# Two layers of 32 experts on one core: experts with one block mixed evenly among those with more, and the overflow loop in two passes behind another expert

## The chip, the core and the metric

The kernel runs on one NeuronCore of a Trainium2 chip. The metric is the device time of one execution in microseconds (us). The core has five engines that are named here by the profile's names: PE (TensorE, with PEld for its weight loads), DVE (VectorE), ACT (ScalarE), POOL (GpSimd) and SP (SyncE, which here issues the large DMA transfers). Each has its own instruction stream; they wait for each other on semaphores.

## The reference

The program is a trunk of two layers on 512 tokens of width 1024, all in float32. Each layer has a mixer (attention in layer 0, a gated linear recurrence in layer 1) and then a mixture of 32 experts of which every token takes two. This change touches only the expert part, which is this:

```python
def moe(xt, idx, wts, w_gu, w_dn):          # xt 512 x 1024, w_gu 32 x 1024 x 1024, w_dn 32 x 512 x 1024
    ...
    def expert_block(args):                 # a block: rows of tokens that chose expert e
        xb, e = args
        g, u = jnp.split(xb @ w_gu[e], 2, axis=-1)
        return (jax.nn.silu(g) * u) @ w_dn[e]
    ...
    return jnp.einsum('tk,tkd->td', wts.astype(y.dtype), y)
```

## The kernel before

**Blocks.** The kernel works in blocks of 32 rows. A fixed plan of 60 blocks per layer gives each expert a number of blocks before the tokens are known: `CAP` gives it by rank. Ranks 0 to 3 are experts 0 to 3 with two blocks each; the other experts are ranked by their number of tokens, and rank 4 has five blocks, rank 5 four, ranks 6 to 8 three, ranks 9 to 19 two, and ranks 20 to 31 one. `RUN` is the order in which the ranks are worked on; a rank's position in it is called its place (0 to 31) here. The blocks are numbered 0 to 59 in that order.

**Work of a block on PE.** Gate and up projections (L1155, 64 matmuls in the trace), the addition to the tokens for a block four earlier (L1182, 32 matmuls), and the down projection of the block before (L1162, 32 matmuls). With each third block of four come 8 transposes of the next four blocks' rows (L1146). Each matmul has a weight load beside it on PEld. The function that does this is the loop over `n` behind `more_blocks()` in the tensor block; ACT, DVE and POOL have loops of the same shape. POOL gathers the rows of four blocks at a time (L714).

**Weights.** An expert's weights are 4 MB (gate and up, "GU") and 2 MB (down, "DN"). There are three sets of buffers, and place n uses set n % 3: set 0 is `ring_gu1`/`ring_dn0`, set 1 `ring_gu0`/`ring_dn1`, set 2 lies in `arena`. `load_expert(n)` on SP (L597 for GU, L599 for DN) waits until the last block of place n - 3 is done with the buffer, and then issues the load. SP issues in the order of the places, all on one DMA queue, GU and DN by turns. A block whose expert has not landed is waited for by PE.

**The overflow loop.** An expert with more tokens than its blocks hold is finished in extra blocks, at most 28, in a loop that all five engines run at one point of the plan: behind block `MORE_BLOCK`, where the buffers of place `MORE_PLACE` = 12 are free (set 0). The count `n_more` is read from memory; an outer loop steps over groups of four extra blocks, and an `If` skips a group that isn't needed. After it, PE counts `more_pe` up, and only then does SP issue the load of place 15. In the profiled execution no extra block ran: the page lists 44 GU loads into `ring_gu` and 18 into `arena`, which are those of 31 places of each layer; place 2 is loaded in parts, and nothing comes on top.

Of the kernel before, what the change touches and what calls it, by code (L numbers as in the profile page):

```python
# [44 lines left out]
MAX_EXTRA = 28  # L45
GROUP = 4
# [6 lines left out]
HEAVY = 20  # L53
# [8 lines left out]
def column(o, j):  # L62
# [3 lines left out]

RUN = ([0, 1, 2, 3, 20, 9, 21, 8, 22, 10, 23, 7, 24, 11, 25, 5, 26, 12, 27, 4, 6]
       + list(range(13, HEAVY)) + [28, 29, 30, 31])
BLOCKS = [(o, j) for o in RUN for j in range(CAP[o])]
NB = len(BLOCKS)  # L70
NU = NB // TILES
assert sorted(RUN) == list(range(NE)) and NB == NU * TILES == sum(CAP)
assert max(column(o, j) for o, j in BLOCKS) < OVCOL
# [15 lines left out]
MORE_PLACE = 12  # L89
MORE_UNIT = 5  # L90
MORE_SET = MORE_UNIT % 2
MORE_BLOCK = TILES * MORE_UNIT + TILES - 1
# [93 lines left out]
def trunk(nc, x, c, positions, norm_mix, norm_ffn, w_ada, b_ada, mla_w_in, mla_q_a_norm, mla_kv_a_norm,  # L186
# [4 lines left out]
    with ctx:  # L191
# [308 lines left out]
        def _(sp):  # L500
# [39 lines left out]
            for l in range(2):  # L540
# [69 lines left out]
                sp.wait_ge(S["dn_done"], gone(MORE_PLACE, l))  # L610
                with sp.Fori(0, MAX_EXTRA // GROUP) as group:
                    with sp.If(n_more > group * GROUP):
                        with sp.Fori(group * GROUP, group * GROUP + GROUP) as u:
                            e = sp.value_load(more_i[0:1, bass.ds(u, 1)], min_val=0, max_val=NE - 1)
                            sp.wait_ge(o["dn_done"], u + 1)
                            sp.dma_start(GU[0].rearrange("p k n -> p (k n)"), gu_rows(l, e)).then_inc(o["w_in"], 16)
                            sp.dma_start(DN[0].rearrange("p k n -> p (k n)"), dn_rows(l, e)).then_inc(o["w_in"], 16)
# [16 lines left out]
        def _(pool):  # L634
# [58 lines left out]
            for l in range(2):  # L693
# [29 lines left out]
                n_more = pool.value_load(more_i[0:1, 31:32], min_val=0, max_val=MAX_EXTRA)  # L723
                with pool.Fori(0, MAX_EXTRA // GROUP) as group:
                    with pool.If(n_more > group * GROUP):
                        with pool.Fori(group * GROUP, group * GROUP + GROUP) as u:
                            g.tensor_copy(idx_in[0:ROWS, :], tok_idx[0:ROWS, bass.ds(u + OVCOL, 1)]).then_inc(o["idx"], 1)
# [13 lines left out]
        def _(pe):  # L741
# [283 lines left out]
            for l in range(2):  # L1025
# [177 lines left out]
                def more_blocks():  # L1203
                    o = OV[l]
                    pe.wait_ge(S["more_ready"], l + 1)
                    n_more = pe.value_load(more_i[0:1, 31:32], min_val=0, max_val=MAX_EXTRA)
                    with pe.Fori(0, MAX_EXTRA // GROUP) as group:
                        with pe.If(n_more > group * GROUP):
                            with pe.Fori(group * GROUP, group * GROUP + GROUP) as u:
                                pe.wait_ge(o["gathered"], u * 16 + 16)  # L1210
# [70 lines left out]
        def _(act):  # L1281
# [181 lines left out]
            for l in range(2):  # L1463
# [93 lines left out]
                u = 2 * l + 1  # L1557
# [34 lines left out]
                def more_blocks():  # L1592
# [3 lines left out]
                    n_more = act.value_load(more_i[0:1, 31:32], min_val=0, max_val=MAX_EXTRA)  # L1596
                    with act.Fori(0, MAX_EXTRA // GROUP) as group:
                        with act.If(n_more > group * GROUP):
                            with act.Fori(group * GROUP, group * GROUP + GROUP) as ub:
                                act.wait_ge(o["xT_made"], ub + 1)  # L1600
# [26 lines left out]
        def _(dve):  # L1627
# [364 lines left out]
            for l in range(2):  # L1992
# [81 lines left out]
                u = 2 * l + 1  # L2074
# [201 lines left out]
                def more_blocks():  # L2276
                    o = OV[l]
                    dve.wait_ge(S["more_ready"], l + 1)
                    n_more = dve.value_load(more_i[0:1, 31:32], min_val=0, max_val=MAX_EXTRA)
                    with dve.Fori(0, MAX_EXTRA // GROUP) as group:  # L2280
                        with dve.If(n_more > group * GROUP):
                            with dve.Fori(group * GROUP, group * GROUP + GROUP) as ub:
                                dve.wait_ge(o["sil"], ub + 1)
# [100 lines left out]
```

## Time and profile before

| | us |
|---|---|
| median of 3 runs | 1695.38 |
| the three runs | 1690.26, 1695.38, 1696.04 |
| profiled execution, own time | 1690.38 |
| its span | 1688.6 |
| expert part of layer 0, about | 400 to 914 of the span |
| expert part of layer 1, about | 1183 to 1688 of the span |

The profile is of one execution; all times of rows are from the start of its span. The profiled execution's time is 1.8 us more than its span, and 5.0 us less than the median.

### The profile page before, as it was taken

To read this page: it belongs to the slowest core of one execution; us is meant where nothing else is said; L and a number is where in the kernel's file an instruction comes from. 1 tells how busy PE (TensorE), PEld (TensorE's weight loads), DVE (VectorE), ACT (ScalarE), POOL (GpSimd) and SP (SyncE) were. 2 spreads that over 40 slices of the span, in tenths; PEclk is the share of its full clock that TensorE was granted. 3 is DMA by queue.
4 is the path that set the end of the run, shared out by engine and by line. 5 is a ranking of instruction groups with operands and counts; after the bars stand their busy time and mean duration, and the time that the engine had idled before them with its cause. 6 is when DMAs were issued, how large, how long until landed. Compare 5 with 4: busy or idle time off the path is not lost.

```text
span 1688.6 us, 40579 instructions
## 1 busy us (share of the span) xinstructions
PE 1545.8 (92%) x17779; PEld 894.6 (53%) x17779; DVE 974.5 (58%) x1632; ACT 349.0 (21%) x708; POOL 175.9 (10%) x212
## 2 busy tenths in 40 slices
PE   3999999989998869899998999897999889899997
PEld 2654555445565536566655444343566446566664
DVE  4677777666555325455555378756565435455555
ACT  2346555131100001001002144613100000000100
POOL 1002211000101001001000122200010000100100
PEclk9999999989999989999999999998999989999999
DMA  9553332499999989979996122047799999998995
GB/s 363 232 231 141 109 98 89 158 345 389 386 401 404 407 319 395 402 309 394 413 429 240 50 75 75 25 187 311 308 404 387 403 399 408 397 353 356 407 424 240
DMA packets 59959, 500.96 MB, mean 297 GB/s; under 512 B 9557, under 2 KB 22290, under 8 KB 43146
## 3 DMA queue, kind: packets, MB, share of 16 engines
q1 hardware_dynamic: 50544, 485.38, 72.4%
q0 software_dynamic: 5088, 7.81, 1.5%
q10 hardware_dynamic: 4154, 5.18, 0.9%
q8 instruction: 143, 2.34, 0.6%
q14 instruction: 30, 0.25, 0.0%
HBM read 497.89 MB, written 6.32 MB: 299 GB/s over the span
## 4 chain that ended last, share of the span: by engine, by line
PE 77%; DMA 11%; DVE 7%; issue 2%; ACT 2%; SPq 1%; DVEq 0%; ACTq 0%
PE ps L1155 23%; PE ps L1182 12%; PE ps L1162 11%; PE ps L1047 6%; DMA arena<-in_moe_w_gu_dram 4%; DMA ring_gu<-in_w_ada_dram 4%; PE ps L1080 3%; DMA ring_gu<-in_moe_w_gu_dram 3%; PE ps L964 3%; PE ps L1066 2%; PE ps L1104 2%; PE ps L874 2%; PE ps L984 2%; PE ps L938 2%; PE ps L854 2%
## 5 line engine op out<-in xcount | busy, mean ns | idle before, releaser
L2303 DVE TENSOR_TENSOR x_tok<-x_tok,ps 128x1024 f32<-128x1024 f32 x240 | 282.6, 1218 | 108.8 <-PE ps L1182 108.2
L1155 PE MATMUL ps<-ring_gu,arena 128*32 128x256 f32 x5248 | 311.0, 387 | 35.9 <-issue 21.2
L1155 PEld LDWEIGHTS ps<-ring_gu,arena 128*32 128x32 f32 x5248 | 171.0, 112 | 155.4 <-issue 35.7
L2095 DVE TENSOR_TENSOR arena<-arena,ps 128x128 f32<-128x128 f32 x120 | 34.5, 288 | 342.5 <-ACT arena L1622 342.4
L1622 ACT ACTIVATE arena<-ps 128x128 f32<-128x128 f32 x120 | 33.3, 278 | 890.2 <-PE ps L1155 890.2
L1182 PE MATMUL ps<-arena 32*128 32x256 f32 x2880 | 195.5, 385 | 4.2 <-DVE arena L2312 3.0
L714 POOL DMA_INDIRECT arena<-xn_dram,tok_idx x104 | 94.7, 911 | 933.2 <-PE ps L1146 594.3
L1162 PE MATMUL ps<-ring_dn,arena 128*32 128x256 f32 x2624 | 159.3, 384 | 4.6 <-DVE arena L2100 2.5
L1182 PEld LDWEIGHTS ps<-arena 32*128 32x128 f32 x2880 | 143.1, 186 | 35.5 <-issue 23.1
L1155 PE MATMUL ps<-arena 128*32 128x256 f32 x2432 | 142.8, 387 | 19.1 <-DMA arena<-in_moe_w_gu_dram 15.9
L1155 PEld LDWEIGHTS ps<-arena 128*32 128x32 f32 x2432 | 78.8, 112 | 75.1 <-DMA arena<-in_moe_w_gu_dram 16.9
L1162 PEld LDWEIGHTS ps<-ring_dn,arena 128*32 128x32 f32 x2624 | 78.2, 110 | 75.7 <-issue 29.8
L1047 PE MATMUL ps<-arena 128*128 128x512 f32 x256 | 110.6, 592 | 0.1
L1182 PE MATMUL ps<-arena,gate_bc 32*128 32x256 f32 x960 | 80.7, 405 | 7.6 <-DVE x_tok L2303 6.3
L1047 PEld LDWEIGHTS ps<-arena 128*128 128x128 f32 x256 | 48.6, 190 | 61.0 <-issue 60.5
L1162 PE MATMUL ps<-arena 128*32 128x256 f32 x1216 | 73.5, 382 | 0.0
L964 PE MATMUL ps<-ring_dn 96*128 96x512 f32 x128 | 66.1, 597 | 0.1
L2089 DVE SCALAR_TENSOR_TENSOR arena<-ps,wtab,gate_bc 128x256 f32<-128x256 f32 x120 | 57.2, 478 | 15.1 <-PE ps L1162 15.1
L1080 PE MATMUL ps<-ring_gu,ring_dn 128*128 128x512 f32 x128 | 57.4, 606 | 5.2 <-ACT arena L1498 5.2
L1182 PEld LDWEIGHTS ps<-arena,gate_bc 32*128 32x128 f32 x960 | 43.8, 185 | 34.5 <-issue 24.5
L1644 DVE SCALAR_TENSOR_TENSOR gate_bc<-ring_gu,c_act,gate_bc 128x1024 f32<-128x1024 f32 x42 | 53.9, 1284 | 9.1 <-DMA ring_gu<-in_w_ada_dram 7.8
L1868 DVE TENSOR_REDUCE mla_small<-ps 128x1 f32<-128x512 f32 x64 | 44.0, 688 | 25.1 <-PE ps L964 24.9
(355 smaller groups left out, 1742.0 us busy)
## 6 DMA issues: line engine op xcount, KB each, us to landing
ring_gu<-in_moe_w_gu_dram SPq DMA_DIRECT2D x44, 4096.0 KB, 18.5
ring_dn<-in_moe_w_dn_dram SPq DMA_DIRECT2D x43, 2048.0 KB, 16.6
arena<-in_moe_w_gu_dram SPq DMA_DIRECT2D x18, 4096.0 KB, 25.3
arena<-in_moe_w_dn_dram SPq DMA_DIRECT2D x20, 2048.0 KB, 19.1
ring_gu<-in_w_ada_dram SPq DMA_DIRECT2D x12, 2048.0 KB, 20.5
ring_gu<-in_w_ada_dram SPq DMA_DIRECT2D x48, 512.0 KB, 4.8
arena<-in_rnn_w_in_dram SPq DMA_DIRECT2D x8, 1024.0 KB, 7.2
arena<-in_moe_w_gu_dram SPq DMA_DIRECT2D x3, 2048.0 KB, 19.8
```

The source lines that it names most:

```text
L714: g.indirect_dma_start(xg[part, :], None, xn_dram, bass.IndirectOffsetOnAxis(ap=tok_idx[0:ROWS, col:col + 1], axis=0), bounds_check=SEQ - ...
L964: mm(ps[:, 2 + qt, :], qT[0:QK, hb, qt * P:(qt + 1) * P], kT[0:QK, hb, :], start=True, stop=True).then_inc(S["s_ready"], 1)
L1047: last = mm(bank(g), w[:, k, m * P:(m + 1) * P], hT[:, k, :], start=(k == 0), stop=(k == KT - 1))
L1080: last = mm(bank(g), yT[:, k, i * P:(i + 1) * P], w_o[:, k, hf * HALF:(hf + 1) * HALF], start=(k == 0), stop=(k == KT - 1))
L1155: last = mm(ps[s_ * ROWS:(s_ + 1) * ROWS, pb, 0:2 * QF].rearrange("p (a b) -> p a b", a=2), rows[:, k, :], pair[:, :, s_, :], start=(k == ...
L1162: last = mm(ps[s_ * ROWS:(s_ + 1) * ROWS, pb, 0:QD], src[:, f * ROWS:(f + 1) * ROWS], w[:, f, s_ * QD:(s_ + 1) * QD], start=(f == 0), stop ...
L1182: last = mm(ps[:, bank0 + q, cols * QD:(cols + 1) * QD], hot[part, i * P:(i + 1) * P], rows[part, :], start=(b == 0), stop=(b == len(block ...
L1644: ins = v.scalar_tensor_tensor(out=acc, in0=w, scalar=ck, in1=acc, op0=ALU.mult, op1=ALU.add)
L1868: v.tensor_reduce(nmax[:, p % 4:p % 4 + 1], ps[:, 2 + p % 4, :], AX.X, ALU.max, negate=True).then_inc(S["nmax_ready"], 1)
L2089: v.scalar_tensor_tensor(out=yo[:, n % 4, :], in0=ps[:, dn_bank(n), 0:QD], scalar=wtab[:, col:col + 1], in1=gate_bc[:, 1, l * QD:(l + 1) * ...
L2095: v.tensor_tensor(hmid[:, n % 2, :], hsil[:, n % 2, :], ps[:, gu_bank(n), QF:2 * QF], ALU.mult).then_inc(S["hmid_ready"], 1)
L2303: return v.tensor_tensor(by_quarter, by_quarter, ps[:, bank0:bank0 + TILES, cols * QD:(cols + 1) * QD], ALU.add)
```

## The change

The diff has two parts. The first is a new `RUN`. In ranks with their blocks in parentheses, places 4 to 31 were 20(1) 9(2) 21(1) 8(3) 22(1) 10(2) 23(1) 7(3) 24(1) 11(2) 25(1) 5(4) 26(1) 12(2) 27(1) 4(5) 6(3) 13 to 19 (2 each) 28(1) 29(1) 30(1) 31(1). They are now 20(1) 4(5) 21(1) 22(1) 5(4) 23(1) 9(2) 6(3) 10(2) 24(1) 7(3) 25(1) 11(2) 8(3) 26(1) 12(2) 13(2) 27(1) 14(2) 15(2) 28(1) 16(2) 17(2) 29(1) 18(2) 19(2) 30(1) 31(1).

The second is the overflow loop. `MORE_UNIT` goes from 5 to 6, so that the loop stands behind block 27 instead of block 23; block 27 is now the last of place 12. And the outer loop has two passes (4 and 24 extra blocks) instead of seven of 4, on each of the five engines.

```diff
-RUN = ([0, 1, 2, 3, 20, 9, 21, 8, 22, 10, 23, 7, 24, 11, 25, 5, 26, 12, 27, 4, 6]
-       + list(range(13, HEAVY)) + [28, 29, 30, 31])
+RUN = ([0, 1, 2, 3, 20, 4, 21, 22, 5, 23, 9, 6, 10, 24, 7, 25, 11, 8, 26, 12, 13, 27, 14, 15, 28, 16, 17, 29, 18, 19]
+       + [30, 31])
...
 MORE_PLACE = 12
-MORE_UNIT = 5
+MORE_UNIT = 6
 MORE_SET = MORE_UNIT % 2
 MORE_BLOCK = TILES * MORE_UNIT + TILES - 1
...
-                    with pe.Fori(0, MAX_EXTRA // GROUP) as group:
+                    with pe.Fori(0, 2) as group:
                         with pe.If(n_more > group * GROUP):
-                            with pe.Fori(group * GROUP, group * GROUP + GROUP) as u:
+                            with pe.Fori(group * GROUP, group * (MAX_EXTRA - GROUP) + GROUP) as u:
```

The same three lines change in the streams of SP, POOL, ACT and DVE.

Three places of PE's stream show the move. The first is place 5, in layer 0. L1155 names the GU buffer that a block reads: `arena` is set 2, which place 5 uses. Before, from block 9's down projection on:

```order
L1162 MATMUL ps<-arena 32x256 x16
L1155 MATMUL ps<-ring_gu1,arena 32x256 x32
L1182 MATMUL ps<-arena,gate_bc 128x256 x4
L1182 MATMUL ps<-arena 128x256 x4
L1182 MATMUL ps<-arena,gate_bc 128x256 x4
L1182 MATMUL ps<-arena 128x256 x4
L1162 MATMUL ps<-arena 32x256 x16
L1155 MATMUL ps<-ring_gu0,arena 32x256 x32
```

In the changed kernel the same rows of the stream are:

```order
L1162 MATMUL ps<-arena 32x256 x16
L1155 MATMUL ps<-arena 32x256 x32
L1182 MATMUL ps<-arena,gate_bc 128x256 x4
L1182 MATMUL ps<-arena 128x256 x4
L1182 MATMUL ps<-arena,gate_bc 128x256 x4
L1182 MATMUL ps<-arena 128x256 x4
L1162 MATMUL ps<-arena 32x256 x16
L1155 MATMUL ps<-arena 32x256 x32
```

(In every L1155 row `arena` also holds the rows of the tokens; where it stands alone, it holds the weights too.) Blocks 11 and 12 had been those of places 6 and 7; they are now still those of place 5, whose buffer is in use from block 9 to block 13.

The second is late in the layer, blocks 48 to 50. Before:

```order
L1155 MATMUL ps<-ring_gu1,arena 32x256 x32
L1182 MATMUL ps<-arena 128x256 x16
L1162 MATMUL ps<-arena 32x256 x16
L1155 MATMUL ps<-ring_gu1,arena 32x256 x32
L1182 MATMUL ps<-arena 128x256 x16
L1162 MATMUL ps<-ring_dn0,arena 32x256 x16
L1155 MATMUL ps<-ring_gu0,arena 32x256 x16
```

In the changed kernel:

```order
L1155 MATMUL ps<-ring_gu1,arena 32x256 x32
L1182 MATMUL ps<-arena 128x256 x16
L1162 MATMUL ps<-arena 32x256 x16
L1155 MATMUL ps<-ring_gu0,arena 32x256 x32
L1182 MATMUL ps<-arena 128x256 x16
L1162 MATMUL ps<-ring_dn0,arena 32x256 x16
L1155 MATMUL ps<-ring_gu0,arena 32x256 x16
```

Place 24 (`ring_gu1`) had two blocks here and has one now; place 25 (`ring_gu0`) is reached one block earlier.

The third is the loop's head: L1206 reads `n_more`, L1207 and L1208 are the outer loop and its `If`. Before:

```order
L1155 MATMUL ps<-ring_gu0,arena 32x256 x32
L1182 MATMUL ps<-arena,gate_bc 128x256 x4
L1182 MATMUL ps<-arena 128x256 x4
L1182 MATMUL ps<-arena,gate_bc 128x256 x4
L1182 MATMUL ps<-arena 128x256 x4
L1162 MATMUL ps<-ring_dn0,arena 32x256 x16
L1162 MATMUL ps<-ring_dn1,arena 32x256 x16
L1206 TENSOR_LOAD more_i
```

In the changed kernel, four blocks later:

```order
L1155 MATMUL ps<-ring_gu1,arena 32x256 x32
L1182 MATMUL ps<-arena,gate_bc 128x256 x4
L1182 MATMUL ps<-arena 128x256 x4
L1182 MATMUL ps<-arena,gate_bc 128x256 x4
L1182 MATMUL ps<-arena 128x256 x4
L1162 MATMUL ps<-ring_dn0,arena 32x256 x32
L1206 TENSOR_LOAD more_i
```

Both stand behind the down projection of the last block, which was one of place 13 (`ring_dn1`) and is now one of place 12 (`ring_dn0`), the one whose buffers the loop would use.

## Rows read from the trace of the kernel before

**Rows 1.** The page: PE's busy time; the chain that ended last, by engine

```profile
PE 1545.8 (92%) x17779; PEld 894.6 (53%) x17779; DVE 974.5 (58%) x1632; ACT 349.0 (21%) x708; POOL 175.9 (10%) x212
...
PE 77%; DMA 11%; DVE 7%; issue 2%; ACT 2%; SPq 1%; DVEq 0%; ACTq 0%
```

**Rows 2.** PE's waits in layer 0, 430 to 914 us: total, times, longest

```profile
PE ps L1155 <- issue: 14.2, 1, 14.2
PE ps L1155 <- DMA arena<-in_moe_w_gu_dram: 8.8, 1, 8.8
PE ps L1155 <- DMA ring_gu<-in_moe_w_gu_dram: 7.9, 3, 5.3
```

**Rows 3.** Timeline of PE, layer 0: start, length, and idle time before

```profile
466.76 3.64 PE L1155 MATMUL ps<-arena 128*32 128x256 f32 x64
...
474.02 1.91 PE L1155 MATMUL ps<-arena 128*32 128x256 f32 x32
...
482.50 3.64 PE L1155 MATMUL ps<-ring_gu,arena 128*32 128x256 f32 x64
...
521.96 3.66 PE L1155 MATMUL ps<-ring_gu,arena 128*32 128x256 f32 x64 [1.76 <-DMA ring_gu<-in_moe_w_gu_dram]
...
537.52 1.93 PE L1155 MATMUL ps<-ring_gu,arena 128*32 128x256 f32 x32 [0.84 <-DMA ring_gu<-in_moe_w_gu_dram]
...
555.00 5.22 PE L1155 MATMUL ps<-arena 128*32 128x256 f32 x64 [8.78 <-DMA arena<-in_moe_w_gu_dram]
...
563.84 3.64 PE L1155 MATMUL ps<-arena 128*32 128x256 f32 x64
...
595.37 1.93 PE L1162 MATMUL ps<-ring_dn,arena 128*32 128x256 f32 x32 [1.10 <-DVE arena L2089]
611.54 5.95 PE L1155 MATMUL ps<-ring_gu,arena 128*32 128x256 f32 x64 [14.24 <-issue]
...
692.61 3.64 PE L1155 MATMUL ps<-ring_gu,arena 128*32 128x256 f32 x32 [5.27 <-DMA ring_gu<-in_moe_w_gu_dram]
...
703.65 3.64 PE L1155 MATMUL ps<-ring_gu,arena 128*32 128x256 f32 x64
...
869.56 3.64 PE L1155 MATMUL ps<-arena 128*32 128x256 f32 x64
```

**Rows 4.** The same in layer 1 (the first and last row are cut by their windows)

```profile
1249.53 0.83 PE L1155 MATMUL ps<-arena 128*32 128x256 f32 x12
...
1385.37 6.44 PE L1155 MATMUL ps<-ring_gu,arena 128*32 128x256 f32 x64 [6.94 <-issue]
...
1642.25 1.05 PE L1155 MATMUL ps<-arena 128*32 128x256 f32 x16
```

**Rows 5.** The If's branch on PE, layer 0, then layer 1: ns min/median/max, first and last start

```profile
L1208 PEldq COMPARE_BRANCH  x7: 221/221/7384, 598.9 to 610.8; - x7
...
L1208 PEldq COMPARE_BRANCH  x7: 221/221/356, 1380.0 to 1384.6; - x7
```

**Rows 6.** SP's issues of GU loads, layer 0: places 15, 21, 26 and 31

```profile
612.12 0.35 SPq L597 DMA_DIRECT2D ring_gu<-in_moe_w_gu_dram  x1
...
688.63 0.64 SPq L597 DMA_DIRECT2D ring_gu<-in_moe_w_gu_dram  x1
...
798.38 0.33 SPq L597 DMA_DIRECT2D arena<-in_moe_w_gu_dram  x1
...
871.05 0.33 SPq L597 DMA_DIRECT2D ring_gu<-in_moe_w_gu_dram  x1
```

**Rows 7.** Those four loads: KB, us from issue to landing

```profile
ring_gu<-in_moe_w_gu_dram SPq DMA_DIRECT2D x1, 4096.0 KB, 13.5
...
ring_gu<-in_moe_w_gu_dram SPq DMA_DIRECT2D x1, 4096.0 KB, 36.2
...
arena<-in_moe_w_gu_dram SPq DMA_DIRECT2D x1, 4096.0 KB, 15.6
...
ring_gu<-in_moe_w_gu_dram SPq DMA_DIRECT2D x1, 4096.0 KB, 20.1
```

More of the change, by code:

```diff
@@ L610, in _ @@
                 sp.wait_ge(S["dn_done"], gone(MORE_PLACE, l))
-                with sp.Fori(0, MAX_EXTRA // GROUP) as group:
+                with sp.Fori(0, 2) as group:
                     with sp.If(n_more > group * GROUP):
-                        with sp.Fori(group * GROUP, group * GROUP + GROUP) as u:
+                        with sp.Fori(group * GROUP, group * (MAX_EXTRA - GROUP) + GROUP) as u:
                             e = sp.value_load(more_i[0:1, bass.ds(u, 1)], min_val=0, max_val=NE - 1)
@@ L723, in _ @@
                 n_more = pool.value_load(more_i[0:1, 31:32], min_val=0, max_val=MAX_EXTRA)
-                with pool.Fori(0, MAX_EXTRA // GROUP) as group:
+                with pool.Fori(0, 2) as group:
                     with pool.If(n_more > group * GROUP):
-                        with pool.Fori(group * GROUP, group * GROUP + GROUP) as u:
+                        with pool.Fori(group * GROUP, group * (MAX_EXTRA - GROUP) + GROUP) as u:
                             g.tensor_copy(idx_in[0:ROWS, :], tok_idx[0:ROWS, bass.ds(u + OVCOL, 1)]).then_inc(o["idx"], 1)
@@ L1596, in more_blocks @@
                     n_more = act.value_load(more_i[0:1, 31:32], min_val=0, max_val=MAX_EXTRA)
-                    with act.Fori(0, MAX_EXTRA // GROUP) as group:
+                    with act.Fori(0, 2) as group:
                         with act.If(n_more > group * GROUP):
-                            with act.Fori(group * GROUP, group * GROUP + GROUP) as ub:
+                            with act.Fori(group * GROUP, group * (MAX_EXTRA - GROUP) + GROUP) as ub:
                                 act.wait_ge(o["xT_made"], ub + 1)
@@ L2279, in more_blocks @@
                     n_more = dve.value_load(more_i[0:1, 31:32], min_val=0, max_val=MAX_EXTRA)
-                    with dve.Fori(0, MAX_EXTRA // GROUP) as group:
+                    with dve.Fori(0, 2) as group:
                         with dve.If(n_more > group * GROUP):
-                            with dve.Fori(group * GROUP, group * GROUP + GROUP) as ub:
+                            with dve.Fori(group * GROUP, group * (MAX_EXTRA - GROUP) + GROUP) as ub:
                                 dve.wait_ge(o["sil"], ub + 1)
```

## The prediction

> **What bounds the kernel now.** I read the page first. PE is busy for 92% of the span and holds 77% of the chain that ended last; DMA holds 11% of it [rows 1]. So the kernel is bound by PE, with stretches in which PE waits for weights. The change touches only the expert parts, so I next read PE's waits there. In layer 0 there are two kinds [rows 2]: one wait of 14.2 us that nothing in the profile ends ("issue"), and 16.7 us for expert weights. The timeline says where they stand [rows 3]. PE waits 1.76, 0.84 and 8.78 us before blocks 16, 18 and 19, the first blocks of places 9, 10 and 11. It waits 14.24 us at the overflow loop, and 5.27 us before block 34, the first of place 19. Layer 1 has the same loop wait at 6.94 us [rows 4].
>
> Two rates set all this. Without a wait, PE needs 7.26 us for a block and 8.48 us for each third one (466.76 to 474.02 to 482.50 [rows 3]): 30.26 us for four. The loads run in one queue. With the queue full, I take place 15's landing (612.12 + 13.5 = 625.6) and place 21's (688.63 + 36.2 = 724.8): 16.5 us per expert over six. The starts of places 9 and 11 that ended waits, 521.96 and 555.00, also lie 2 x 16.5 apart [rows 3, 6, 7]. Late in the layer, places 26 (814.0) and 31 (891.1) lie 15.4 us per expert apart. So an expert with one block takes PE 7 to 8 us and the queue about 16; one with two blocks keeps both about equal; one with more gives the queue time. Sixty blocks are 454 us of PE, 29 loads at 16 us are 464 us. The two resources are almost equally loaded over a layer, and mixing can win only what one of them idles.
>
> **The loop.** PE's seven branches on the `If` start from 1380.0 to 1384.6 in layer 1 [rows 5]: 0.77 us per pass. Five passes fewer are 3.8 us per layer, and they lie on the path, because PE does nothing else there and the load of place 15 is issued 0.6 us after PE goes on (611.54, 612.12). POOL's, SP's, DVE's and ACT's passes are saved beside PE's and count nothing. In layer 0 the first branch took 7.384 us, in layer 1 0.356 us [rows 5]; that is 7.0 us which the loop's work does not explain, and the trace of before can't say whether it stays when the loop moves. Bounds: nothing, or -7.0 us. Thirteen of fourteen branches are short, but the long one is the very branch that is moved; I take -4.
>
> **The new order, before the loop.** Place 5 now has five blocks, 9 to 13. The load of place 8 waits for block 13, at 466.76 + 30.26 + 3.6 = 500.6 us instead of about 479. From an empty queue it takes 13.5 us [rows 7] and lands at 514; block 16 is due at 520. Places 9 to 11 follow at 16.5 us: 531, 547, 564, for blocks due at 550, 557 and 573. So the three waits before the loop go (11.4 us), and the slow start behind them too: block 19 took 8.84 us instead of 7.26 [rows 3].
>
> Block 28 is due at 466.76 + 144.0 = 610.8. What does the loop's place cost? Before, block 24 was due at 466.76 + 113.8 + 11.4 + 1.6 = 593.5 and started at 611.54: 18.0 us. With 3.8 less, block 28 starts at 625.0. In layer 1 the same with 7.0 us less for the branch: 1249.53 + 144.0 + 7.2 = 1400.8 [rows 4].
>
> **The new order, behind the loop.** Place 15 is issued at 625.6 and lands at 639.1. From there the queue never empties, so the landings are a sum. Up to place 22 I take 16.2 us per expert. The two measured values are 16.5 and 15.4; it is near the first, which comes from the same places, but the experts there now hold 12 blocks instead of 18. Place 22 lands at 639.1 + 7 x 16.2 = 752.5. Its first block, 44, is due at 625.0 + 2.1 + 121.0 = 748.1 (2.1 is the slow start behind a wait, the mean of 1.6 above and 2.6 for block 34, which took 11.04 us instead of 8.48 [rows 3]). So PE waits 4.4 us. From here on three experts have five blocks: 37.5 us of PE against 3 x 15.4 = 46.2 us of loads. Place 25 lands at 798.7, block 49 is due at 792.1: 6.6 us. Place 28 lands at 844.9, block 54 is due at 838.3: 6.6 us. Block 57 then starts at 844.9 + 2.1 + 23.0 = 870.0. Before, it started at 869.6 [rows 3]: +0.4 us, the loop's 3.8 us included. Behind block 57 both orders have the same work, and place 31 lands in time in both.
>
> Layer 1: place 15 lands at 1401.4 + 13.5 = 1414.9, place 22 at 1528.3, place 28 at 1620.7, block 57 starts at 1645.8, against 1642.3 before [rows 4]: +3.5 us.
>
> **Sum.** +0.4 + 3.5 - 4 = 0 us. The waits before the loop and at place 19 are removed, and three waits late in each layer come in their place, because before, experts with two blocks stood in a row there, 15.1 us of PE each beside 15.4 us of load, and now one in three is a single block. The profiled execution took 1690.4 us, 5.0 us less than the median of the three runs, which spread over 5.8 us; I name 1694. A measurement of this kernel can tell 0.5% (8.5 us) from no change.
>
> **Rivals.**
> *The queue gains from the mixing (faster).* If the late rate of 15.4 us holds from place 15 on, place 22 lands at 746.9 without a wait, place 28 at 839.3, and block 57 starts at 864.4: -5.2 us. Layer 1: -2.1 us. With -4 for the branch that is -11.3 us, 1684 us. For it: the long experts, whose gathers fill the queue besides the weights, are gone from the stretch. Against it: 16.5 us was measured just there.
> *The queue becomes the bound to the end (slower).* If 16.5 us holds for all 13 loads from place 16 to 28, block 57 starts at 639.1 + 214.5 + 25.1 = 878.7, +9.1 us, and in layer 1 +12.2 us: 1717 us, or 1713 with the branch's gain. It decides from a mean of 16.2 us per load on, where the sum is +8.5. For it: the queue is now full for 13 loads on end, and before, late in the layer, SP issued at PE's pace. Against it: the late experts are the same ones, and they took 15.4 us.
> *The branch.* In layer 0 the first branch is short now (-3 us against the sum), or stays long (+4), or layer 1 gets a long one too (+11). None of the first two leaves the 0.5%.
> Beside this stands the Trainium skill, "Runtime: NRT & Kernel Launch", section "Instruction fetch mechanics": instructions are fetched in blocks of 256, one after the other, and a taken branch whose target isn't among the two blocks at hand has to wait for a fetch. By that rule the 7.4 us depend on where the branch lies in its block of 256, and moving the loop by four blocks decides them anew; the sum would be -3 us with a short branch. The trace agrees so far that the same branch in the same loop costs 7.384 and 0.356 us.
>
> **How the numbers follow.** My sum 0.50; the branch's other outcomes 0.15; the queue gains 0.20; the queue bounds 0.15. The range leaves out the far ends of the last two: 1683 to 1709. Faster by over 0.5% 0.20, within 0.65, slower 0.15. The likeliest case alone reaches from 1687 to 1700 us.
>
> **What would show it.** In the new trace PE should have no wait for weights between 430 us and the loop, a loop wait near 3 us in layer 1, two branches per layer at L1208, and three waits of 4 to 7 us before the first blocks of places 22, 25 and 28 (all `ring_gu0`). Place 8 should be issued near 501 us. The sum is wrong if place 28 does not land near 845 and 1621 us: each 0.1 us in the rate is 2.6 us in the time. It is also wrong if an early wait comes back because the queue, empty for some 8 us before place 8, does not catch up.

## The result, and the profile after

| | before | after |
|---|---|---|
| median, us | 1690.93 (20 runs, 1685.12 to 1696.04) | 1694.76 (20 runs, 1688.53 to 1700.78) |
| ratio to before | | 1.0021, 95% interval 1.0012 to 1.0030 |
| profiled execution | 1690.38 | 1694.73 (span 1693.0) |

The changed kernel is slower by 0.21%, 3.6 us. The page of the changed kernel, PE's busy time and the chain that ended last by engine:

```profile
PE 1544.3 (91%) x17779; PEld 894.4 (53%) x17779; DVE 974.3 (58%) x1632; ACT 348.8 (21%) x708; POOL 175.4 (10%) x212
...
PE 73%; DMA 16%; DVE 7%; ACT 2%; issue 2%; SPq 0%; DVEq 0%; ACTq 0%
```

PE's work is the same (1545.8 us in [rows 1]); the chain has moved from PE to DMA, from 11% to 16%. PE's waits of the changed kernel, first in layer 0 (430 to 914 us), then in layer 1 (1215 to 1692 us), as total, times and longest:

```profile
PE ps L1155 <- DMA ring_gu<-in_moe_w_gu_dram: 22.6, 3, 9.8
PE ps L1155 <- issue: 8.4, 1, 8.4
...
PE ps L1155 <- DMA ring_gu<-in_moe_w_gu_dram: 22.0, 3, 8.7
...
PE ps L1155 <- issue: 3.3, 1, 3.3
```

Against [rows 2] the loop wait of layer 0 is 5.8 us shorter and the weight waits are 5.9 us longer (22.6 against 8.8 + 7.9). In layer 1 the loop wait is 3.6 us shorter and the weight waits are 7.9 us longer (22.0 against 7.2 + 6.9); these are PE's waits of before in layer 1, same window:

```profile
PE ps L1155 <- DMA arena<-in_moe_w_gu_dram: 7.2, 1, 7.2
...
PE ps L1155 <- DMA ring_gu<-in_moe_w_gu_dram: 6.9, 3, 4.8
```

The timeline of PE says where (start, length, wait before it); the last row of each layer is block 57:

```profile
622.16 5.05 PE L1155 MATMUL ps<-ring_gu,arena 128*32 128x256 f32 x64 [8.37 <-issue]
...
752.99 6.18 PE L1155 MATMUL ps<-ring_gu,arena 128*32 128x256 f32 x64 [9.76 <-DMA ring_gu<-in_moe_w_gu_dram]
...
799.51 5.12 PE L1155 MATMUL ps<-ring_gu,arena 128*32 128x256 f32 x64 [6.28 <-DMA ring_gu<-in_moe_w_gu_dram]
...
845.27 3.64 PE L1155 MATMUL ps<-ring_gu,arena 128*32 128x256 f32 x32 [6.59 <-DMA ring_gu<-in_moe_w_gu_dram]
...
870.62 3.64 PE L1155 MATMUL ps<-arena 128*32 128x256 f32 x64
...
1401.34 3.66 PE L1155 MATMUL ps<-ring_gu,arena 128*32 128x256 f32 x64 [3.34 <-issue]
...
1529.54 5.33 PE L1155 MATMUL ps<-ring_gu,arena 128*32 128x256 f32 x64 [8.70 <-DMA ring_gu<-in_moe_w_gu_dram]
...
1622.26 3.32 PE L1155 MATMUL ps<-ring_gu,arena 128*32 128x256 f32 x32 [6.27 <-DMA ring_gu<-in_moe_w_gu_dram]
...
1646.67 3.64 PE L1155 MATMUL ps<-arena 128*32 128x256 f32 x64
```

No weight wait stands before the loop any more, and three stand before blocks 44, 49 and 54, the first of places 22, 25 and 28. Block 57 starts 1.1 us later than in [rows 3] in layer 0 and 4.4 us later than in [rows 4] in layer 1 (3.1 of them within the expert part, which began 1.3 us later). The landings come from SP's issues and the time from issue to landing, places 15, 22 and 28 of layer 0, then 22 and 28 of layer 1:

```profile
622.64 0.34 SPq L597 DMA_DIRECT2D ring_gu<-in_moe_w_gu_dram  x1
716.44 0.33 SPq L597 DMA_DIRECT2D ring_gu<-in_moe_w_gu_dram  x1
813.34 0.33 SPq L597 DMA_DIRECT2D ring_gu<-in_moe_w_gu_dram  x1
1494.28 0.34 SPq L597 DMA_DIRECT2D ring_gu<-in_moe_w_gu_dram  x1
1590.63 0.33 SPq L597 DMA_DIRECT2D ring_gu<-in_moe_w_gu_dram  x1
```

```profile
ring_gu<-in_moe_w_gu_dram SPq DMA_DIRECT2D x1, 4096.0 KB, 13.4
ring_gu<-in_moe_w_gu_dram SPq DMA_DIRECT2D x1, 4096.0 KB, 36.3
ring_gu<-in_moe_w_gu_dram SPq DMA_DIRECT2D x1, 4096.0 KB, 31.9
ring_gu<-in_moe_w_gu_dram SPq DMA_DIRECT2D x1, 4096.0 KB, 35.0
ring_gu<-in_moe_w_gu_dram SPq DMA_DIRECT2D x1, 4096.0 KB, 31.6
```

So they land at 636.0, 752.7, 845.2, 1529.3 and 1622.2 us: 16.7 us per load (GU and DN of one expert) from place 15 to 22 in layer 0, and 15.4 and 15.5 from 22 to 28 in the two layers. Place 15 of layer 1 lands at 1415.1 us, which makes 16.3 us per load to place 22 there. The branch on the `If`, layer 0 and layer 1 (min, median and max in ns, first and last start), as [rows 5] of before:

```profile
L1208 PEldq COMPARE_BRANCH  x2: 227/2724/5221, 615.4 to 621.3; - x2
...
L1208 PEldq COMPARE_BRANCH  x2: 221/332/444, 1399.4 to 1400.4; - x2
```

### The profile page after: what moved, and what is told of

Its sections match the earlier page's. It is cut to its first block, busy times and chain, and to the rows that moved or that the text cites. A ratio compares the mean times of both kernels' runs of the same rounds, so it can differ in the third digit from the quotient of the medians.

```text
span 1693.0 us, 40379 instructions
## 1 busy us (share of the span) xinstructions
PE 1544.3 (91%) x17779; PEld 894.4 (53%) x17779; DVE 974.3 (58%) x1632; ACT 348.8 (21%) x708; POOL 175.4 (10%) x212
## 4 chain that ended last, share of the span: by engine, by line
PE 73%; DMA 16%; DVE 7%; ACT 2%; issue 2%; SPq 0%; DVEq 0%; ACTq 0%
PE ps L1155 22%; DMA ring_gu<-in_moe_w_gu_dram 12%; PE ps L1182 11%; PE ps L1162 10%; PE ps L1047 6%; DMA ring_gu<-in_w_ada_dram 4%; PE ps L1080 3%; PE ps L964 3%; PE ps L1066 2%; PE ps L1104 2%; PE ps L874 2%; PE ps L984 2%; PE ps L938 2%; PE ps L854 2%; PE ps L902 2%
## 5 line engine op out<-in xcount | busy, mean ns | idle before, releaser
L1155 PE MATMUL ps<-ring_gu,arena 128*32 128x256 f32 x4096 | 248.5, 394 | 56.3 <-DMA ring_gu<-in_moe_w_gu_dram 44.6
L1155 PEld LDWEIGHTS ps<-ring_gu,arena 128*32 128x32 f32 x4096 | 135.2, 114 | 154.5 <-issue 46.6
L1155 PE MATMUL ps<-arena 128*32 128x256 f32 x3584 | 205.9, 379 | 3.2 <-ACT arena L1564 3.2
L1155 PEld LDWEIGHTS ps<-arena 128*32 128x32 f32 x3584 | 114.7, 110 | 80.6 <-ACT arena L1564 3.6
L1162 PE MATMUL ps<-ring_dn,arena 128*32 128x256 f32 x2048 | 123.3, 382 | 4.6 <-DVE arena L2100 2.5
L1162 PE MATMUL ps<-arena 128*32 128x256 f32 x1792 | 109.2, 384 | 0.0
L1162 PEld LDWEIGHTS ps<-ring_dn,arena 128*32 128x32 f32 x2048 | 61.0, 109 | 58.9 <-issue 21.9
L1162 PEld LDWEIGHTS ps<-arena 128*32 128x32 f32 x1792 | 52.9, 110 | 48.3 <-issue 19.5
## 6 DMA issues: line engine op xcount, KB each, us to landing
arena<-in_moe_w_dn_dram SPq DMA_DIRECT2D x20, 2048.0 KB, 16.5
```

The costliest lines, as they stand in the source:

```text
L1155: last = mm(ps[s_ * ROWS:(s_ + 1) * ROWS, pb, 0:2 * QF].rearrange("p (a b) -> p a b", a=2), rows[:, k, :], pair[:, :, s_, :], start=(k == ...
L1162: last = mm(ps[s_ * ROWS:(s_ + 1) * ROWS, pb, 0:QD], src[:, f * ROWS:(f + 1) * ROWS], w[:, f, s_ * QD:(s_ + 1) * QD], start=(f == 0), stop ...
```

## The experiments

Fifteen runs in four sets, each set on another chip and each kernel beside before on its own chip. The changed kernel itself was run again only in set 4 (after_again). On the chip of the first set before took 1692 us, on those of the other three 1717 to 1718 us. Ratios are to before:

| kernel | set | ratio, 95% interval | median, us |
|---|---|---|---|
| e_passes | 1 | 0.9977 (0.9965 to 0.9989) | 1686.73 |
| e_order | 1 | 1.0044 (1.0029 to 1.0060) | 1698.87 |
| e_pad_before | 1 | 0.9964 (0.9947 to 0.9981) | 1686.00 |
| e_pad_after | 1 | 1.0000 (0.9987 to 1.0013) | 1691.87 |
| e_tail | 2 | 0.9931 (0.9915 to 0.9947) | 1705.25 |
| e_five | 2 | 0.9931 (0.9915 to 0.9947) | 1705.43 |
| e_best | 2 | 0.9911 (0.9892 to 0.9930) | 1700.17 |
| e_nogather | 2 | 0.9860 (0.9841 to 0.9878) | 1691.91 |
| e_best_again | 3 | 0.9900 (0.9875 to 0.9924) | 1700.53 |
| e_tail_again | 3 | 0.9937 (0.9914 to 0.9961) | 1707.93 |
| e_late | 3 | 0.9967 (0.9952 to 0.9982) | 1712.44 |
| e_pad_after2 | 3 | 1.0001 (0.9985 to 1.0018) | 1719.11 |
| e_early | 4 | 0.9933 (0.9909 to 0.9956) | 1705.90 |
| after_again | 4 | 1.0021 (1.0006 to 1.0035) | 1720.13 |
| e_best_third | 4 | 0.9914 (0.9897 to 0.9932) | 1702.19 |

### The two passes alone, and the order alone

```diff
 e_passes, against before (on all five engines)
-                    with pe.Fori(0, MAX_EXTRA // GROUP) as group:
+                    with pe.Fori(0, 2) as group:
...
 e_order, against the changed kernel (on all five engines)
-                    with pe.Fori(0, 2) as group:
+                    with pe.Fori(0, MAX_EXTRA // GROUP) as group:
```

> Before's order of ranks and before's place of the loop, only its outer loop in two passes (4 and 24 blocks) on all five engines. My theory: each of the five passes that go costs PE 0.77 us on the path in each layer, since place 15's load is issued only when the loop is over and the stretch behind it is bound by that load; the loop wait goes from 14.2 to about 10.4 us in layer 0 (the long first branch of 7.4 us stays, because no instruction of the static program moves) and from 6.9 to about 3.1 us in layer 1; the time falls by 7.7 us (ratio 0.9955). Rival 1, the passes are hidden by the queue of loads: no change. Rival 2, the long first branch goes as well: -14.7 us.

> The changed kernel with the outer loop in seven passes of 4 again: the new order of ranks and the loop's new place alone. My theory: the order and the place cost what the two passes give and 3.6 us more: +11.3 us against before (ratio 1.0067), +7.7 us against the changed kernel; the three late waits stay at about 9, 6 to 7 and 6 to 7 us in each layer. Rival 1, the passes count nothing where the loop now stands (the loads of places 13 and 14 are still in the queue while PE is in the loop): +3.6 us against before, as the changed kernel. Rival 2, the waits of the changed kernel come from the shorter loop, which starts place 15's load against gathers that it did not meet before: then they shrink here and the kernel is at +0 to +4 us.

Both sides give the same value: the passes are worth 3.9 us (e_passes against before, 1.9 to 5.9 by its interval; 1.0044 against 1.0021, with some 3 us of uncertainty), half of the 7.7 expected; the order and the loop's place cost 7.4 us. PE of e_passes at the loop and before block 26, the first of place 15, layer 1:

```profile
1377.57 6.51 PE L1155 MATMUL ps<-ring_gu,arena 128*32 128x256 f32 x64 [3.17 <-issue]
...
1396.22 2.89 PE L1155 MATMUL ps<-ring_gu,arena 128*32 128x256 f32 x32 [2.81 <-DMA ring_gu<-in_moe_w_gu_dram]
```

The loop wait fell by 3.8 us as expected, but a wait of 2.81 us that before does not have came in two blocks later. Place 15's load is issued at 1378.1 us, while those of place 14 are still in the queue (they land at 1381.1 and 1386.5), and it takes 18.0 us instead of 14.4. Counted from block 7 to block 57, layer 1 of e_passes is 0.7 us longer than that of before, and layer 0 is 4.1 us shorter (the loop wait is 9.76 us instead of 14.24, of which 0.7 us is the branch). In the changed order this loss does not show: from block 7 to block 57 layer 1 took 415.0 us in e_order and 410.4 us in the changed kernel, and layer 0 took 420.4 and 418.6 us (with a branch 1.4 us longer in the latter). That is 6.5 us in two profiles; why the ratios give only 3.9 us on that side is open.

### Where the branch's time comes from

```diff
-            pe.wait_ge(S["pool_const"], 1)
+            for _ in range(170): pe.wait_ge(S["pool_const"], 1)
```

(e_pad_before: 170, in before. e_pad_after: 60, e_pad_after2: 170, in the changed kernel.)

> Before, with 170 waits that are already fulfilled put at the start of PE's stream, where PE idles for over 20 us anyway; nothing else is changed, only each later instruction of PE lies 170 places further on in the program. Theory (position): the 7.4 us of the first branch at L1208 in layer 0 come from where the branch lies in the program's pieces of 256 instructions. Its position modulo 256 is about 207 in layer 0 and 38 in layer 1; with 170 more it is 121 and 208. So layer 0's first branch becomes short (under 1 us) and layer 1's long (7.4 us), and the time changes by less than 2 us. Rival 1, the branch is long because it is the first execution of the loop in the program: layer 0's stays at 7.4 us, layer 1's at 0.4 us. Rival 2, the data of the count comes late in layer 0: the same rows as rival 1.

> The changed kernel with 60 fulfilled waits at the start of PE's stream. The first branch at L1208 lies at about 231 and 61 modulo 256 in the changed kernel; with 60 more at 35 and 121. Theory (position): both layers have short branches (under 1 us), layer 0's loses 4.8 us of its 5.2, place 15's load is issued as much earlier, and since loads bound what follows, the time falls by 4.8 us against the changed kernel: -1.2 us against before (ratio 0.9993). Rival, the long branch comes from the first execution of the loop: 5.2 us stay and the time is the changed kernel's, +3.6 us.

> The changed kernel with 170 fulfilled waits at the start of PE's stream instead of 60. In the six profiles so far the first branch is long (3.8 to 7.4 us) where the last fetch of instructions by PE lies 7.6 to 10.1 us before it, and short (under 0.5 us) where it lies 2.5 to 4.4 us before. Theory: 60 waits moved it only from 8.7 to 10.1 us; 170 carry it past the next fetch, so that the branch of layer 0 is short, and the time is 4.8 us less than the changed kernel's (ratio 0.9993 to before). Rival, in the changed kernel the branch stays long whatever lies in front: 3.8 to 5.2 us, ratio 1.000 to 1.002.

The branch of e_pad_before in layer 0:

```profile
L1208 PEldq COMPARE_BRANCH  x7: 221/221/460, 601.8 to 606.7; - x7
```

The 7.4 us of layer 0 are gone and the kernel is 6.1 us faster, so neither "first execution" nor late data explains them (both rivals had the 7.4 us stay). But the same run kept layer 1's branch short (445 ns), where the position modulo 256 said 7.4 us, and in e_pad_after 3.9 of 5.2 us stayed. The arithmetic of positions, my theory, fell. e_pad_after is 3.5 us faster than the changed kernel all the same; its branch explains 1.3 of them, the rest is open (the intervals of the two are 1.5 and 2.2 us wide to each side). What took the theory's place came from two executions of one program. Layer 0 of e_tail and of e_tail_again, which are the same kernel; first the branch of each, then PE's instruction queue, q8, in the 9.5 us before the first branch of e_tail_again (in the same stretch of e_tail no row of that queue stands):

```profile
L1208 PEldq COMPARE_BRANCH  x2: 233/2068/3902, 630.0 to 634.4; - x2
```

```profile
L1208 PEldq COMPARE_BRANCH  x2: 227/348/468, 634.4 to 635.4; - x2
```

```profile
q8 instruction: 1, 0.02, 0.9%
```

One transfer of 16 KB of instructions, 2.6 us ahead of the branch, goes with the difference between 3.9 and 0.47 us. The distance to it sorts all 34 first branches of the 17 profiles: 12 of them are long (3.3 to 7.4 us), all in layer 0, and there that queue's last transfer began 7.4 to 11.0 us earlier; at the 22 short ones it began 2.2 to 6.7 us earlier. A long branch ends 2.3 to 2.6 us after the next transfer begins (before: 4.9 us into the branch, which took 7.384), as it would if it waited for that one; no run moves the transfer alone, so this is a sorting and not a proof. What sets the moment of the transfer is open. In before the last transfer lies 8.8 us ahead in layer 0 and 3.2 in layer 1. In e_pad_after2 the branch came out as its theory has it, the last transfer at 4.3 us and the branch at 379 ns; its time, 1.0001 (0.9985 to 1.0018), fits the theory (0.9993) and the rival (1.000 to 1.002) alike. And since after_again, without waits added, also had a short one on the chip of the fourth set (468 ns), that run alone proves little. Beside it stands the Trainium skill, "Runtime: NRT & Kernel Launch", section "Instruction fetch mechanics": a taken branch whose target is not among the blocks at hand waits for a fetch. The trace agrees so far that long branches end shortly after a transfer of that queue; that the position in the program alone decides it does not hold here.

### What the gathers cost the queue

```diff
                 for t in range(MORE_UNIT + 2, NU):
-                    gather(t)
+                    pool.wait_ge(S["xT_made"], NU * l + t)
+                    for q in range(TILES):
+                        part = slice(q * ROWS, (q + 1) * ROWS)
+                        g.dma_start(xg[part, 0:16], xn_dram[part, 0:16]).then_inc(S["gathered"], 16)
```

> The changed kernel without the gathers of groups 8 to 14 (the rows of blocks 32 to 59; in their place four transfers of 16 columns each): it leaves out fetching these blocks' rows, which stay those of earlier blocks. Theory (the gathers take their time from the load queue): from place 15 to 22 a load takes 15.0 us instead of 16.3 to 16.7, PE does not wait before block 44, and the waits before places 25 and 28 stay at 5 to 6 us each; -22 us against the changed kernel (ratio 0.989 to before). Rival, the loads are slow there by themselves or by PE's and ACT's reads and writes: 16.3 us stay, and the time is that of the changed kernel within 3 us.

Place 22's load of layer 0, issued at 722.45 us, and its time to landing; place 15's was issued at 628.75 us and took 13.3 us:

```profile
722.45 0.33 SPq L597 DMA_DIRECT2D ring_gu<-in_moe_w_gu_dram  x1
```

```profile
ring_gu<-in_moe_w_gu_dram SPq DMA_DIRECT2D x1, 4096.0 KB, 26.6
```

Seven loads took 749.1 - 642.1 = 107.0 us, 15.3 us each instead of 16.7, and in layer 1 14.9 instead of 16.3. But the changed kernel's values are from another chip. On this one e_tail, which has the changed kernel's order up to block 52, needs 16.5 and 16.1 us per load from place 15 to 22 (649.3 to 764.8 and 1440.1 to 1552.9 us), so the gathers take 1.2 us per load from the queue. From place 22 to 28 a load takes 15.1 us in e_nogather, so without gathers the queue has nearly one rate all through.

The wait before block 44 is only 0.24 us. That doesn't tell of the gathers: e_tail on this chip and after_again on that of set 4 have the gathers and no wait of 0.5 us or more there either; PE reaches block 44 later on these chips, since its blocks are slower (below). The waits before blocks 49 and 54 stay at 5.96 and 5.86 us: these come from three places having five blocks, not from the gathers. The kernel is 27.6 us faster than the changed one at its 1.0021, more than the 22 expected. Against after_again, place 28 lands 14.1 us earlier in each layer, counted from block 7; about 11.5 us of that come after place 15's landing and the rest before it, where PE is faster by pauses that are missing (below).

### Which part of the order costs

```diff
 places 15 to 31 of the changed kernel
-25, 11, 8, 26, 12, 13, 27, 14, 15, 28, 16, 17, 29, 18, 19, 30, 31
 e_tail: rank 29 to place 29
+25, 11, 8, 26, 12, 13, 27, 14, 15, 28, 16, 17, 18, 19, 29, 30, 31
 e_early: before's kind of late part behind place 18
+25, 11, 8, 26, 12, 27, 13, 14, 15, 16, 17, 18, 19, 28, 29, 30, 31
...
 e_late: places 20 to 31 of e_passes
-6, 13, 14, 15, 16, 17, 18, 19, 28, 29, 30, 31
+6, 13, 14, 28, 15, 16, 29, 17, 18, 19, 30, 31
...
 e_five: RUN of the changed kernel, rank 4 (five blocks) from place 5 to place 21
-       [0, 1, 2, 3, 20, 4, 21, 22, 5, 23, 9, 6, 10, 24, 7, 25, 11, 8, 26, 12, 13, 27, 14, ...
+       [0, 1, 2, 3, 20, 21, 22, 5, 23, 9, 6, 10, 24, 7, 25, 11, 8, 26, 12, 13, 27, 4, 14, ...
-MORE_UNIT = 6
+MORE_UNIT = 5
```

> The changed kernel with one rank moved: the single-block rank 29 goes from place 27 behind ranks 18 and 19, to place 29; everything up to block 52 is as it is. Theory (the last landing that PE waits for sets the end, plus the blocks that are left behind it): place 28 lands as before near 845 and 1621 us, but its first block is then block 55 instead of 54, so 5 blocks are left behind the wait instead of 6. Block 57 starts 7.3 to 8.5 us earlier in each layer, place 29's load has landed by then: -16 us against the changed kernel, -12 us against before (ratio 0.993). Rival 1, the queue is the bound to the end: block 57, now the first of place 29, waits for a load that lands 15.4 us behind place 28's, and the single blocks behind it wait as well; nothing to -4 us against the changed kernel. Rival 2, the early part of the new order is what costs: no change.

> The kernel of e_tail once more, beside e_best_again on the same chip. Theory: -16 us against the changed kernel, 0.9925 to before on a chip without the pauses, because the wait before block 54 is not in its way and one block fewer stands behind the last landing waited for.

> Before's order up to place 20 and before's place of the loop, then the changed kernel's kind of mixing for the rest (2 2 1, 2 2 1, 2 2 2, 1 1 instead of seven twos and four ones), loop in two passes: e_passes with the late part mixed. Theory (the late mixing costs only where the queue is behind; before's early part leaves it a lead of 6 us at place 22 and the late experts hold the same 22 blocks in all): the same as e_passes within 1 us, 0.9977 to before, with at most 1 us of wait before places 25 and 28. Rival, three places with five blocks cost 46.2 - 37.5 = 8.7 us each wherever they stand: waits of 5 us or more before places 25 and 28, +10 us or more against e_passes.

> The changed kernel up to place 17 (26), then before's kind of late part: 12 27, seven twos in a row, then 28 29 30 31 as the last four; the same loop behind block 27. Theory (neither part costs by itself; what ends the layer is the last landing that PE waits for, plus the blocks behind it, and a queue that is behind is answered best by twos in a row and singles last): a wait of 5 to 6 us before place 21, under 1 us each before places 24 to 27, and 7 us before place 29, block 57's; 16 us less than the changed kernel, 12 us less than before (ratio 0.9928). Rival 1, the early part costs (idle queue before place 8, loop later): as the changed kernel, 1.002 to before, whatever stands behind. Rival 2, late mixing costs nothing anywhere (as in e_late): also as the changed kernel.

> The changed kernel itself, as the baseline of this set. On a chip without pauses 1.002 to before; on one with the pauses of PE behind the gathers less than that, since it has 20 us of weight waits per layer that can take them up, and before has 8 to 9 us less: 0.997 to 1.000.

> The changed kernel with the five-block rank 4 moved from place 5 to place 21, and the loop therefore behind block 23 again (still the last block of place 12 or before). Theory (idle time of the load queue is never made up): place 8 is issued near 475 us instead of 501, so the queue does not run empty before it; a new wait of 7 to 9 us comes before place 7, and the waits before places 25 and 28 go, since five blocks of PE lie beside the queue's work late in the layer. -18 us against the changed kernel, -15 us against before (ratio 0.991), more of it in layer 0 (-13) than in layer 1 (-5). Rival 1, the queue's idle time early in the layer is harmless, the late pattern of singles costs: then the waits of layer 0 and 1 add up to as much as in the changed kernel, +0 to +4 us against before. Rival 2, the loop's place behind block 23 costs (the loads of places 13 and 14 are not queued then): PE waits over 5 us before place 15 or 16.

The four combinations with two passes, as ratios to before:

| | late part of before's kind | late part mixed |
|---|---|---|
| early part of before | 0.9977 (e_passes, set 1) | 0.9967 (e_late, set 3) |
| early part of the changed kernel | 0.9933 (e_early, set 4) | 1.0021 (after_again, set 4, and the first result) |

The lower row is one chip and shows most: the late part alone makes 15 us. The new early part with twos in a row behind it is 11.5 us faster than before. The late mixing costs nothing behind the old early part: e_late has no wait for weights from place 22 on. Only both together are slow. Two things limit this. e_passes ran on the chip of set 1 alone, where PE's blocks are faster and so wait more; neither e_late nor e_early was run there. And e_late mixes two single blocks among the twos, at places 23 and 26, where the changed kernel has three. e_early's waits in layer 0 from 640 us on, and then those of after_again, the changed kernel on the same chip, from 430 us on:

```profile
PE ps L1162 <- issue: 5.8, 13, 0.8
PE ps L1155 <- DMA arena<-in_moe_w_gu_dram: 3.8, 1, 3.8
```

```profile
PE ps L1155 <- DMA ring_gu<-in_moe_w_gu_dram: 9.0, 2, 6.2
```

One weight wait of 3.8 us is left (place 29's), where the changed kernel has 9.0 us on this chip, and 22.6 us in its first profile; in layer 1 it is 1.7 against 8.3 us. In the first profile of the changed kernel the queue is behind from place 22 on, in after_again from place 25 on, and each single block among twos adds a wait, the last at place 28 with six blocks still to do. e_tail has the same experts with one single block moved behind the twos, and is 11.8 us (in e_tail_again 10.8 us) under before. The number came out, but not the way the expectation had it. Its last wait for weights stands before block 49, not before the first block of place 28:

```profile
813.38 3.21 PE L1155 MATMUL ps<-ring_gu,arena 128*32 128x256 f32 x28 [6.55 <-DMA ring_gu<-in_moe_w_gu_dram]
```

Block 54 is now one of place 27, and PE works on it while place 28 lands (858.65 us; its first block starts at 864.45). after_again waits before block 49 as well (6.22 us, and 3.54 in layer 1 against 4.16 in e_tail) and once more before block 54 (2.77 and 4.75 us). So what e_tail saves is that second wait with the slow start behind it. From block 7 to block 57 e_tail_again, whose branch is as short as after_again's, is 3.9 us shorter in layer 0 and 7.3 in layer 1; the two ratios are 14 us apart, so some of the gain is not seen in these two executions.

e_five is 11.8 us faster than before instead of the 15 expected: a wait of 2.9 us before place 7 in layer 0, where 7 to 9 were expected, and none late. Its blocks are slower, by the pauses of the next part. after_again missed its expectation (0.997 to 1.000): the ratio is 1.0021 there as well.

### An order searched with the measured rates

```diff
-RUN = ([0, 1, 2, 3, 20, 4, 21, 22, 5, 23, 9, 6, 10, 24, 7, 25, 11, 8, 26, 12, 13, 27, 14, 15, 28, 16, 17, 29, 18, 19]
+RUN = ([0, 1, 2, 3, 20, 9, 12, 26, 4, 21, 10, 25, 23, 8, 6, 19, 14, 27, 15, 11, 17, 5, 29, 16, 7, 22, 13, 28, 18, 24]
...
-MORE_UNIT = 6
+MORE_UNIT = 5
```

> Another order, searched by a recurrence of PE's blocks and the queue's loads that was fitted to the two traces (10.0 us for a GU load, 5.0 for a DN load, 4.4 us times the share of rows for a gather of four blocks): in blocks per place from place 4 on 1 2 2 1 5 1 2 1 1 3 3 2 2 1 2 2 2 4 1 2 3 1 2 1 2 1 1 1, loop in two passes behind block 23. Theory (what counts is that the queue never runs empty and PE never waits; the last places are short): the expert waits of a layer sum to under 8 us, block 57 near 847 us in layer 0, -41 us against the changed kernel, -37 us against before (ratio 0.978). Rival 1, the queue slows down when it is full all the time (16.5 us per load instead of about 15.5): the gain is halved, -15 to -20 us. Rival 2, PE is the bound as the page says (92% busy), order gives at most the 11 us of waits of a layer: -10 us.

> The kernel of e_best once more. On the chip that e_best ran on, a block of PE took 7.96 us in the mean (767.1 to 806.9 for five) instead of 7.51, with three pauses of 0.7 us of PE about 3 us after each group of gathers, which the profiles of before and of the changed kernel do not have. Theory: e_best has no weight waits, so it is bound by PE's blocks and pays for these pauses in full (53 blocks by 0.4 us per layer), while before has room for part of them; on a chip without them it is at 0.978 to before. If the pauses are there again, 0.991. Rival, the order itself gives no more than 0.9% on any chip: 0.991 without pauses.

> The kernel of e_best a third time. On a chip without the pauses of 0.7 us behind the gathers 0.978 to before; with them 0.990 to 0.991 as twice before. Rival, the order gives 0.9% everywhere: 0.991 without pauses.

It is faster than before in all three sets, by 0.9 to 1.0% (15 to 17 us), and 18 us faster than the changed kernel in the one set that has both (set 4), but the 2.2% expected did not come. PE's waits of e_best in the expert part of layer 0, and PE between two groups of blocks there:

```profile
PE ps L1155 <- issue: 10.3, 3, 9.3
PE ps L1162 <- issue: 9.9, 23, 0.8
```

```profile
788.43 0.94 PE L1162 MATMUL ps<-ring_dn,arena 128*32 128x256 f32 x8
789.70 1.09 PE L1162 MATMUL ps<-ring_dn,arena 128*32 128x256 f32 x3 [0.33 <-issue]
791.11 1.26 PE L1162 MATMUL ps<-ring_dn,arena 128*32 128x256 f32 x17 [0.33 <-issue]
```

There is no weight wait left at all. What holds the kernel back are 23 short stops of PE which nothing in the profile ends. They come in groups of two or three, 3 to 6 us after POOL issues the first of the four gathers of a group (issued from 785.5 to 789.1 us here), in all kernels of sets 2 to 4 and in none of set 1 or of the first two profiles. In e_nogather they stand behind the gathers that are left (480 to 486 us, 512 to 517 us) and are missing where those were taken out. That they go with the gathers is shown; why only some chips have them is not. Four blocks take 32.5 us in e_best (684.2 to 846.7 us for twenty) instead of 30.26, so a group of stops costs about 2.2 us. Part of that lies within PE's busy time (1564.9 us against 1544.3 in the changed kernel's first profile) and part in its idle time (9.9 us in layer 0). There are 26 groups of gathers in the two layers, by which the stops would cost a kernel that never waits some 50 to 60 us, as an estimate. A kernel that waits for loads hides part of them: before became 25 us longer from the first set's chip to these. So most of what e_best lacks to its 0.978 can be the stops, but the account can't be closed, because e_best never ran on a chip without them, and before was not profiled on one with them.

## Why the prediction was wrong

**The step that failed is "I take -4" for the branch, a gain that the sum carries whole to the end of layer 0.** Without it, its own terms sum to +0.4 + 3.5 = 3.9 us, and the kernel became 3.6 us slower. Layer 1, where no such term was in the sum, came out as worked out: block 57 3.1 us later within the expert part against 3.5. In layer 0 the branch shortened by 2.2 us only (7.384 to 5.221), and none of that reached the end: block 57 started 1.1 us later than before, where +0.4 - 4 = -3.6 was forecast.

**Why the 2.2 us were lost there.** The rate from place 15 to 22 was 16.7 us per load instead of the 16.2 taken, 3.3 us over seven loads. Place 15 landed at 636.0 us instead of 639.1, but place 22 at 752.7, as predicted (752.5): the early start was spent before the first wait. So the 16.2 is the second term that was mis-sized. That place 22 landed on the predicted microsecond is luck: the 3.1 us of early start, which the sum of the landings left out, and the 3.3 us of the rate cancel. With it, it is luck that 3.9 and 3.6 us lie so close. In layer 1 the rate was 16.3 and the landings fit without such luck; why layer 0 is 0.4 us per load slower is open. e_nogather and e_tail show what the rate is made of: about 15.3 us, and 1.2 for the gathers. The step "near the first, but fewer blocks" leaned the wrong way in layer 0.

The wait before block 44 was 9.76 us instead of 4.4, and 8.70 in layer 1, where the same 4.4 follow from the prediction's terms. The load was on time, and PE was early. In part this is a wrong step in the prediction's due time: it gives sixteen blocks 2.1 + 121.0 us behind the loop, and they took 121.1 in layer 0 and 119.5 in layer 1. The down projection of block 27 stands ahead of the loop, so block 28 has none before its additions. It cost nothing, since the landing ends the wait.

**The landings late in the layer were right**, in layer 0 by the cancelling just told: place 28 at 845.2 and 1622.2 us against 844.9 and 1620.7. So were the waits before places 25 and 28 (6.28 and 6.59 us against 6.6 each), the rate of 15.4, the loop wait of layer 1 (3.34 us), the absence of waits before the loop, and place 8 (issued at 500.67 us). The rival that the queue gains and the rival that it bounds to the end both did not come. (The times of these rivals are counted from the median of 1695.4 us, while the sum of 0 us is put at 1694.)

**"Five passes fewer are 3.8 us per layer, and they lie on the path"** was half right. The loop wait fell by that, but e_passes and e_order put the whole at 3.9 us for both layers instead of 7.7; in layer 1 of before's order a wait for place 15 takes most of it back, in the changed order no row shows such a loss. The order costs the rest, 7.4 us.

**The account of the late mixing** (three places with five blocks are 8.7 us of wait each) is right only where the queue is behind: e_late has two such groups of three places and no late wait, on a chip where PE is slower. The prediction looked at the two halves of the order in turn and never asked which partner each needs.

## What to carry to other kernels

When two resources are almost equally loaded, do not price an order by its waits. For each transfer add the work that stands behind it to its landing; the latest of these sums sets the end. Then move long work in front of that transfer and short work behind it, and work the sums out again, because another transfer can now be the one (in e_tail it went from place 28 to place 25). Time saved ahead of a stretch that is bound by the queue counts only as far as the queue starts earlier and keeps its rate, so a gain there is carried to the next wait before it is put in a sum. Compare waits only between profiles of one chip: the changed kernel has 22.6 us of weight waits in layer 0 on one and 9.0 on another, at the same ratio to before. And a stall that two executions of the same program do not share (here a branch of 0.5 or 3.9 us) belongs in the range, not in the sum.

## What the runs showed of the hardware

- The first of PE's branches over the loop's body took 0.36 to 0.47 us, or 3.3 to 7.4 us in the 12 of 34 cases in which the last transfer of PE's instruction queue lay over 7 us before it; the same program had 3.9 us in one execution and 0.47 us in another.
- On the chips of sets 2 to 4, and not on that of set 1, PE loses about 2.2 us behind each group of four gathers (32.5 us for four blocks in e_best against 30.26 in before; PE busy 1573.1 us in after_again against 1544.3 us for the same kernel at first), at about the same granted clock (0.976 and 0.966 of full); without the gathers the stops are missing (e_nogather). The cause is not known.
- A 6 MB load behind others took 15.3 us (14.9 in layer 1) without gathers beside it in e_nogather, and 16.5 us (16.1) with them in e_tail on the same chip; the gathers of four blocks take about 2.1 us of the queue (1.2 us by seven loads, in which four groups fall).
